# Retention's rotated queries and keys: transposed in 32x32 blocks on VectorE in place of 128x128 on TensorE

## What is computed

```python
qh = _rotate(_heads(q, RET_HEADS, RET_HD), cos, sin)
kh = _rotate(_heads(k, RET_HEADS, RET_HD), cos, sin) * (RET_HD ** -0.5)
...
scores = jnp.einsum('bhnid,bhnjd->bhnij', q, k) * dmat[None, :, None]
o_inner = jnp.einsum('bhnij,bhnje->bhnie', scores, v)
```

## Time and profile before

| | us |
|---|---|
| median of 3 runs | 813.63 (813.58 to 813.74) |
| profiled execution | 813.71 |
| its span | 811.9 |
| TensorE matmul busy | 807.3 |
| VectorE busy | 489.4 |
| ScalarE busy | 419.3 |

### The profile page before, as it was taken

How to read it: one execution, slowest core, us unless ns; L and a number is a source line. 1 busy time by engine, 2 the same in 40 slices (tenths; PEclk the granted TensorE clock), 3 DMA queues, 4 the chain that set the end, 5 groups by cost and what they waited for, 6 DMA issues and landing times.

```text
span 811.9 us, 10608 instructions
## 1 busy us (share of the span) xinstructions
PE 807.3 (99%) x4228; PEld 691.2 (85%) x4228; DVE 489.4 (60%) x659; ACT 419.3 (52%) x579; POOL 33.6 (4%) x36
## 2 busy tenths in 40 slices
PE   9999999999999999999999999999999999999998
PEld 8988888888788888888889888888878888888887
DVE  6764586445854854655685546854656567556563
ACT  8575566456743444433575646573475535344331
POOL 0011000000001001000000200000000010010000
PEclk9999999999999999999999999999999999999999
DMA  8785664443644553566556757544457435545553
GB/s 328 266 301 207 231 198 162 162 130 131 210 157 143 175 173 128 187 202 205 184 183 213 248 198 223 183 149 136 134 171 230 142 128 182 182 133 202 181 184 131
DMA packets 41986, 150.48 MB, mean 185 GB/s; under 512 B 4801, under 2 KB 5313, under 8 KB 41809
## 3 DMA queue, kind: packets, MB, share of 16 engines
q1 hardware_dynamic: 41328, 146.82, 54.7%
q0 software_dynamic: 176, 1.77, 0.5%
q10 hardware_dynamic: 432, 1.22, 0.4%
HBM read 147.69 MB, written 2.10 MB: 184 GB/s over the span
## 4 chain that ended last, share of the span: by engine, by line
PE 97%; ACT 1%; DVE 1%; issue 1%; ACTq 0%; DVEq 0%
PE pair L426 65%; PE pair L371 7%; PE bank L371 6%; PE bank L373 4%; PE pair L373 4%; PE bank L453 3%; PE bank L368 1%; PE bank L724 1%; PE bank L556 1%; PE bank L714 1%; PE bank L354 1%; PE bank L638 1%; PE bank L675 0%; PE bank L603 0%; PE bank L663 0%
## 5 line engine op out<-in xcount | busy, mean ns | idle before, releaser
L1012 DVE TENSOR_TENSOR lo<-raw,hi 128x1024 fp32r<-128x1024 f32 (+3 forms) x272 | 315.6, 1179 | 205.9 <-ACT hi L756 204.1
L756 ACT ACTIVATE hi<-raw 128x1024 fp32r<-128x1024 f32 (+3 forms) x272 | 271.4, 1022 | 183.9 <-PE pair L426 83.7
L426 PE MATMUL pair<-hi,xT_lo 128*128 128x512 f32 (+1 forms) x768 | 295.2, 384 | 0.0
L426 PE MATMUL pair<-lo,xT_hi 128*128 128x512 f32 (+1 forms) x768 | 295.1, 384 | 0.0
L426 PE MATMUL pair<-hi,xT_hi 128*128 128x512 f32 (+1 forms) x768 | 292.7, 391 | 0.1
L426 PEld LDWEIGHTS pair<-hi,xT_hi 128*128 128x128 f32 x768 | 144.4, 188 | 29.1 <-DVE lo L1012 1.8
L426 PEld LDWEIGHTS pair<-hi,xT_lo 128*128 128x128 f32 x768 | 144.1, 188 | 28.1
L426 PEld LDWEIGHTS pair<-lo,xT_hi 128*128 128x128 f32 x768 | 144.5, 188 | 26.4 <-issue 0.3
L371 PE MATMUL pair<-yT,hi 128*128 128x512 f32 x256 | 90.0, 396 | 0.1
L371 PE MATMUL bank<-yT,hi 128*128 128x512 f32 x224 | 79.0, 395 | 0.0
L373 PE MATMUL bank<-yT,lo 128*128 128x256 f32 x256 | 71.4, 279 | 0.0
(11 more groups left out here) (146 smaller groups left out, 567.4 us busy)
## 6 DMA issues: line engine op xcount, KB each, us to landing
raw<-stream SPq DMA_DIRECT2D x272, 512.0 KB, 4.2
xT<-x_in SPq DMA_DIRECT2D x8, 256.0 KB, 6.9
consts<-consts_in POOLq DMA_DIRECT2D x1, 1664.0 KB, 8.3
out<-xT SPq DMA_DIRECT2D x3, 512.0 KB, 6.9
mats<-mats_in ACTq DMA_DIRECT2D x2, 576.0 KB, 5.5
out<-xT SPq DMA_DIRECT2D x4, 128.0 KB, 1.8
consts<-consts_in POOLq DMA_DIRECT2D x1, 64.0 KB, 4.2
gains_all<-gains_in ACTq DMA_DIRECT2D x1, 40.0 KB, 3.3
```

Of the source, the lines that this page charges most:

```text
L426: return nc.tensor.matmul(pair[a][m][:, 0:width], x_part[:, slots[i], m * P:(m + 1) * P], w_part[r][:, i * 512:i * 512 + width], start=(sl ...
L756: nc.scalar.activation(cut[0], cut[1], ACT.Copy).then_inc(rounded[r].sem, 1)
L1012: nc.vector.tensor_tensor(cut[0], cut[1], cut[2].bitcast(F32), ALU.subtract).then_inc(split[r].sem, 1)
```

## The change

The 16 transposes of a layer on TensorE and the four ScalarE copies that moved their results out of PSUM go away. VectorE gets a helper `turn_blocks`. A VectorE transpose turns 32x32 blocks; the 128x128 transpose is put together from them by reading from partitions 32i to 32i+31 and writing to partitions 32j to 32j+31. One instruction covers one pair (i, j) for all 4 heads and both token halves: 32 partitions x 256 elements, 8 blocks. So each of the two tensors needs 16 instructions, written straight to `qT_a` or `kT_a` in SBUF. They come in batches of four, with one split ahead of each batch where one is still open. The order on VectorE becomes: `lo_tiles`, batch, split 92, batch, split 93, batch, split 94, batch, `turn_heads` for the keys with splits 95 and 96, batch, split 97, batch, split 98, batch, split 99, batch, split 100, decay. TensorE computes the scores one granule later, after granule 98 and not after 97, and waits there for all 32 instructions.

```diff
-        aq_filled, qT_a_ready = signal("aq_filled", 2), signal("qT_a_ready", 2)
-        ak_filled, kT_a_ready = signal("ak_filled", 2), signal("kT_a_ready", 2)
+        qT_a_ready = signal("qT_a_ready", 16)
+        kT_a_ready = signal("kT_a_ready", 16)
...
                 turn_y(2, gate0, yB_filled)
-                granules(92)
-
-
-                pe.wait_ge(*rq_turned.at(l, 2))
-                for f in range(2):
-                    turn(f, [rq_rot[:, m * HEADS + h, :] for h in (2 * f, 2 * f + 1)
-                             for m in range(MT)]).then_inc(aq_filled.sem, 1)
-                granules(95)
-                pe.wait_ge(*rk_turned.at(l, 2))
+                granules(99)
                 pe.wait_ge(*yTB_ready.at(l, 4))
-                for f in range(2):
-                    turn(2 + f, [rk_rot[:, m * HEADS + h, :] for h in (2 * f, 2 * f + 1)
-                                 for m in range(MT)]).then_inc(ak_filled.sem, 1)
-                granules(98)
+                pe.wait_ge(*qT_a_ready.at(l, 16))
+                pe.wait_ge(*kT_a_ready.at(l, 16))
                 for h in range(HEADS):
-                    if h % 2 == 0:
-                        pe.wait_ge(*qT_a_ready.at(l, h // 2 + 1))
-                        pe.wait_ge(*kT_a_ready.at(l, h // 2 + 1))
...
-                splits(94)
-                for f in range(2):
-                    act.wait_ge(*aq_filled.at(l, f + 1))
-                    nc.scalar.activation(qT_a[:, 2 * f:2 * f + 2, :].rearrange("p h t -> p (h t)"), bank[f][:],
-                                         ACT.Copy).then_inc(qT_a_ready.sem, 1)
-                splits(97)
-                for f in range(2):
-                    act.wait_ge(*ak_filled.at(l, f + 1))
-                    nc.scalar.activation(kT_a[:, 2 * f:2 * f + 2, :].rearrange("p h t -> p (h t)"), bank[2 + f][:],
-                                         ACT.Copy).then_inc(kT_a_ready.sem, 1)
...
-                dve.wait_ge(*rq_turned.at(l, 2))
-                turn_heads(z_rk, z_rk_ready, rk_rot, rk_turned, 92)
-
-                splits(100)
+                def turn_blocks(rot, rotated, dst, ready, at):
+
+
+                    dve.wait_ge(*rotated.at(l, 2))
+                    for j in range(4):
+                        splits(at + j)
+                        for i in range(4):
+                            nc.vector.transpose(
+                                dst[32 * j:32 * j + 32].rearrange("p h (m i t) -> p m i h t", m=MT, i=4)[:, :, i],
+                                rot[32 * i:32 * i + 32].rearrange("p (m h) (j c) -> p m j h c", m=MT, j=4)[:, :, j]
+                                ).then_inc(ready.sem, 1)
+
+                turn_blocks(rq_rot, rq_turned, qT_a, qT_a_ready, 92)
+                turn_heads(z_rk, z_rk_ready, rk_rot, rk_turned, 95)
+                turn_blocks(rk_rot, rk_turned, kT_a, kT_a_ready, 97)
+
+                splits(101)
```

## The result

| | before | changed |
|---|---|---|
| median, us | 813.61 (4 runs) | 825.38 (823.58 to 826.87, 4 runs) |
| profiled execution, us | 813.71 | 825.28 |
| its span, us | 811.9 | 823.4 |

The change makes the kernel slower: ratio 1.0144, 95% interval 1.0129 to 1.0159. The forecast was 822.7 with a range of 814 to 832.

What follows compares the result with a forecast made beforehand. TensorE was taken to bound the kernel, with VectorE's queue making it wait before the scores: 813.7 plus 2 x 4.5 us, the 1.80 a layer from removed transposes already counted, gives 822.7 us, range 814.0 to 832.

Steps and rivals of the forecast that it cites:

- What bounds it: TensorE, busy 807.3 of 811.9 us, bounds the kernel; time given to VectorE is free until it falls behind.
- the sum's first step: Both layers: TensorE's transposes removed and nothing making it wait, the result would be 810.1 us.
- 3.6 us off TensorE: Two groups of eight transposes a layer, two layers, 0.90 us a group, removed from TensorE.
- ScalarE and DMA at nothing: The removed ScalarE copies, and raw-buffer DMAs that wait for later splits, were both costed at nothing.
- The price of a transpose, 0.455 us: Time between starts of VectorE transposes before the scores: 0.42 us plus 0.035, range 0.21 to 0.71.
- the nearest row: VectorE's two-input operation on 256 elements per partition in the earlier profile, 416 ns, taken as a transpose's duration.
- the second kind of distance between starts: VectorE operations that change their half of the partitions: no overlap and 0.03 us of gap.
- the other kind: Transposes overlapping like adds, starts 0.34 us apart: +0.8 us a layer, total 815.3; chance 0.12.
- The estimate from the Trainium skill: From its 311 ns for a VectorE transpose of 128 bf16 columns: 0.48 us each, total near 824.
- The reckoning: VectorE's queue in layer 0 from 272.70: 28.41 us to the last key transpose, scores 6.3 us late, +4.5 a layer.
- Rival 4: TensorE's clock falls to 1.2 GHz in the new holes: some 11 us higher, near 834; chance 0.04.
- The faster side: Transposes two elements at a time fit VectorE's idle time: 810.1 or 814.1; chance 0.10, 0.06 of it clearly faster.

Runs made afterwards that it cites:

- its twin: The changed kernel with the two transpose loops exchanged, so a batch of four reads the same 32 partitions and writes to four different ones: 823.51 us.

## Why the prediction was right, and where it was off

**What bounds it.** Right, and shown: leaving out the transposes, moving one split and taking half of the transposes each came out at the time that VectorE's queue gives, within 0.2 us. TensorE's chain came first, then VectorE's queue in the stretch. Leaving the transposes out gave the 810.1 of the sum's first step to the tenth; "3.6 us off TensorE" measured 3.5.

**ScalarE and DMA at nothing.** Right: in the changed kernel TensorE's waits name VectorE alone, and VectorE itself waits for nothing between 272.66 and the scores.

**The price of a transpose, 0.455 us.** It is 0.465: a duration of 436 ns where the nearest row, had 416, and the same 0.03 of gap. The reason for taking the second kind of distance between starts, the change of partitions seen in the earlier trace rows, was right and carried the forecast: with the other kind the sum gave 815.3, and the kernel whose batches don't change partitions is at 816.9 (it still changes them from batch to batch). The estimate from the Trainium skill ("VectorE: DVE Perf Modes", section "The three transpose paths"), 0.48 us and "near 824", was as near: by its 311 ns for 128 elements and 1.04 ns for each of 128 more an estimate is 444, against 436 measured. In time, 32 x 0.01 x 2 = 0.6 us too little.

**The reckoning.** Forecast: last transpose at 301.11, scores at 301.2; measured 301.42 and 301.56. Holes forecast as 0.4, 0.4, 1.6, 0, 1.5, 0.4 and 2.2; measured as 0.24, 0.25, 1.53, 0, 1.30, 0.26 and 2.22 us. The small ones are shorter than forecast for two reasons: TensorE starts 0.05 us after the end of a split and not 0.1, and the reckoning had every granule at 2.72 us, while one behind a hole takes 2.88. This second error was free: VectorE's 3.1 us a step set the pace, so a slower granule only shortened the hole behind it. It is why the scores are 301.56 - 294.90 = 6.7 us late though the holes sum to 5.8. Forecast +4.5 us a layer; measured +4.94: 0.3 by the transposes, 0.1 because the scores behind a hole take 3.34 us and not 3.26. With the clock at full speed the kernel takes 823.4 to 823.6, so that the queue's part of the forecast, 822.7, was 0.8 short, 0.6 of it in the transposes.

**The clock.** Rival 4 was right in kind and wrong in two numbers. I had given it 0.04, and it came in 4 of the 12 executions of this kernel and its twin, in three of the first four, which is why the median on record is 825.38 and not 823.5. Its price I had put at two granules at half speed, 5.4 us a layer; one fall costs 5.36 - 3.69 = 1.7. The two errors of the term work against each other: it came far more often than I had thought and costs a third as much. The sum had it at nothing, and that is its mis-sized term: 1.7 of the 2.7 us between forecast and median. Which share of this the median shows is luck: four more executions of the same kernel had no fall and a median of 823.42.

**The faster side.** Its condition, under 0.31 us apart, was named rightly and is not met by these instructions; 0.34 is the mean that they reach even without a change of partitions. What I had not seen is that it can be met per element: double-width instructions cost 0.73 us for what took two, 0.37 for each old one, and two granules more of room do the rest. Two elements at a time they never are: 702 - 436 ns for 256 more elements is 1.04 ns each. The Trainium skill ("Vector Engine (DVE) Microarchitecture Reference", section "Performance modes") doesn't list transposes for that mode, and the trace agrees.

## What to carry to other kernels

Work moved from the engine that bounds a kernel to one that is "60% busy" fits or doesn't fit in a stretch, not on average: add up the receiving engine's queue, with everything in it that stands ahead of the consumer, and compare it with the time at which the bounding engine gets there. If it is over by a few microseconds, look for three things before giving up: fewer and wider instructions, unrelated work that can go behind the deadline, and a later deadline. Here these turned 9.9 us of loss into 4.2 of gain.

## What the runs showed of the hardware

- A VectorE transpose of 32 x 256 float32 takes 436 ns where it changes its block of 32 partitions, on the input's or the output's side alike, and 394 right behind one on the same blocks; starts lie 0.465 and 0.34 us apart. 32 x 512, with a change each time, takes 702 ns. That is about one element per 1.04 ns and partition, as for an add.
- Behind a hole, TensorE's second matmul of 512 columns started 0.34 us after the first, where 0.227 is the rhythm, and the granule of 12 took 2.88 us against 2.72.
- In all executions with waits of 0.8 or 1.2 us ahead of the scores, the clock was granted in full (8 of 8). With a wait of 2.06 us (one in each layer) it fell in 4 of 12, with 2.3 us at least once in 10 of 10. A fall to the 1.2 GHz level cost 1.7 us.
